# Moving layer 1's last eight conditioning units from layer 0's gate stage to the boundary between the two layers

## The reference, cut to what matters

```python
for l in range(DEPTH):
    mod_l = (silu(c) @ ada_w[l] + ada_b[l])          # 1024 x 6144 weights per layer
    mod_c = (silu(c_ctx) @ ada_w[l] + ada_b[l])
    sh1, sc1, g1, sh2, sc2, g2 = split(mod_l, 6)     # six parts of 1024 columns
    ul = rmsnorm(hl, norm_g[l, 0]) * (1 + sc1) + sh1
    mc, ml = token_mixer(uc, ul, w_in[l], ...)       # input projection, four mixers, gates, output projection
    hl = hl + g1 * rmsnorm(ml, norm_g[l, 1])
    vl = rmsnorm(hl, norm_g[l, 2]) * (1 + sc2) + sh2
    hl = hl + g2 * rmsnorm(ffn(vl), norm_g[l, 3])    # dense SwiGLU in layer 0, 8 experts in layer 1
```

## Time and profile before

| | us |
|---|---|
| median of 3 runs | 2219.38 |
| lowest and highest of them | 2215.46 and 5585.45 |
| the profiled execution, its time | 2221.07 |
| its span in the trace | 2219.2 |
| layer 0's gate stage in the trace, about | 313 to 602 |
| boundary of the layers, last feed-forward matmul to first projection matmul | 1023.1 to 1036.7 |
| TensorE busy | 2135.0 (96%) |
| VectorE busy | 1422.2 (64%) |
| ScalarE busy | 1154.7 (52%) |

### The profile page before, as it was taken

How to read it: one execution, slowest core, us unless ns; L and a number is a source line. 1 busy time by engine, 2 the same in 40 slices (tenths; PEclk the granted TensorE clock), 3 DMA queues, 4 the chain that set the end, 5 groups by cost and what they waited for, 6 DMA issues and landing times. The chain is left out here.

```text
span 2219.2 us, 37036 instructions
## 1 busy us (share of the span) xinstructions
PE 2135.0 (96%) x15402; PEld 1749.0 (79%) x15402; DVE 1422.2 (64%) x1999; ACT 1154.7 (52%) x1588; POOL 142.2 (6%) x117
## 2 busy tenths in 40 slices
PE   6999899999999999998988899999999999999997
PEld 4787687777778888886866799778888888888886
DVE  3546663333452222336567566589999999999998
ACT  4253432322342222325445245478888888888886
POOL 0004420000000000000014400010000000000000
PEclk9999999999999999999989999999999999999999
DMA  6510025665623222221200254489999999999995
GB/s 245 211 79 1 3 98 228 254 259 209 265 102 112 95 95 97 94 94 60 96 1 2 80 210 170 161 311 378 390 380 372 387 381 386 379 381 383 375 412 201
DMA packets 68201, 468.07 MB, mean 211 GB/s; under 512 B 7681, under 2 KB 8641, under 8 KB 14017
## 3 DMA queue, kind: packets, MB, share of 16 engines
q1 hardware_dynamic: 62192, 440.55, 51.7%
q10 hardware_dynamic: 4688, 20.93, 2.5%
q0 software_dynamic: 1152, 4.19, 0.5%
HBM read 453.03 MB, written 12.62 MB: 210 GB/s over the span
## 5 line engine op out<-in xcount | busy, mean ns | idle before, releaser
L2371 DVE TENSOR_TENSOR wsp_l<-ring,wsp_h 128x1024 fp32r<-128x1024 f32 x528 | 643.2, 1224 | 48.0 <-ACT wsp_h L1513 13.3
L1513 ACT CAST wsp_h<-ring 128x1024 fp32r<-128x1024 f32 x528 | 555.5, 1054 | 136.5 <-PE bank L709 80.5
L707 PE MATMUL bank<-wsp_h,xTs_h 128*128 128x512 f32 x704 | 283.5, 403 | 0.4 <-DVE wsp_l L2371 0.4
L709 PE MATMUL bank<-wsp_h,xTs_l 128*128 128x512 f32 x704 | 275.6, 392 | 0.0
L708 PE MATMUL bank<-wsp_l,xTs_h 128*128 128x512 f32 x704 | 274.3, 390 | 0.0
L2946 DVE TENSOR_TENSOR dsp_l<-ring,dsp_h 128x1024 fp32r<-128x1024 f32 x66 | 80.9, 1226 | 234.1 <-ACT dsp_h L2014 234.0
L2014 ACT CAST dsp_h<-ring 128x1024 fp32r<-128x1024 f32 x66 | 69.2, 1048 | 249.7 <-PE bank L1389 175.3
L1281 PE MATMUL bank<-u_hi,gsp_h 128*128 128x512 f32 (+1 forms) x512 | 174.3, 341 | 0.0
L1281 PE MATMUL bank<-x_lo,gsp_h 128*128 128x512 f32 (+1 forms) x512 | 172.1, 336 | 0.0
L1281 PE MATMUL bank<-u_hi,gsp_l 128*128 128x512 f32 (+1 forms) x512 | 171.6, 335 | 0.0
L709 PEld LDWEIGHTS bank<-wsp_h,xTs_l 128*128 128x128 f32 x704 | 132.2, 188 | 29.1
(11 more groups left out here) (374 smaller groups left out, 4160.5 us busy)
## 6 DMA issues: line engine op xcount, KB each, us to landing
ring<-in_moe_tiles_dram SPq DMA_DIRECT2D x264, 1024.0 KB, 7.1
ring<-in_ada_tiles_dram SPq DMA_DIRECT2D x48, 1024.0 KB, 9.3
ring<-in_ffn_tiles_dram SPq DMA_DIRECT2D x33, 1024.0 KB, 4.8
ring<-in_gate_tiles_dram SPq DMA_DIRECT2D x32, 1024.0 KB, 6.3
ring<-in_in_tiles_dram SPq DMA_DIRECT2D x22, 1024.0 KB, 5.4
arena<-in_branch_tiles_dram ACTq DMA_DIRECT2D x8, 1024.0 KB, 7.0
ring<-in_out_tiles_dram SPq DMA_DIRECT2D x8, 1024.0 KB, 4.9
x_rows<-arena SPq DMA_DIRECT2D x1, 3584.0 KB, 16.2
```

What stands on the lines that cost most here:

```text
L707: pe.matmul(o, xTs[0][:, kk, :], whi[:, k, :], start=(kk == 0), stop=False)
L709: mm = pe.matmul(o, xTs[1][:, kk, :], whi[:, k, :], start=False, stop=(kk == KD - 1))
L1513: act.copy(wsp[0][:, g % 4, :], half_slot(MOE0, g)).then_inc(s.gq_o.up, 1)
L2371: v.tensor_tensor(wsp[1][:, g % 4, :], half_slot(MOE0, g), wsp[0][:, g % 4, :], ALU.subtract).then_inc(s.gq_pt.up, 1)
```

## The change

The last group of conditioning units leaves the gate stage. Its tiles stand behind the feed-forward's in `slots`, ahead of layer 1's first projection tile. PE does three of the units between the transposes of tiles 0 and 1, and five between those of tiles 1 and 2, all into bank 4, after waiting that `post_add` has read tile 2 out of it (`po_h2(3)`). Then it waits for `ada_copy` before bank 4 is used for transposes. `ada_columns` of this group follows the first projection tile, `modulate_group` goes to DVE's fifth half tile, and layer 1's transposition of its gate rows goes one projection tile later.

```diff
--- before.py
+++ after.py
@@ -46,6 +46,7 @@
 GROUP = 8
 ADA_BATCH = (3, 3, 2)
 ROW_AT = 17
+LAST_AT = 3
 RING = 6
 LEVELS = 5
 CH = 64
@@ -342,7 +343,7 @@
         def ada_batch(g):
 
             i, j = divmod(g, len(ADA_BATCH))
-            return range(GROUP * i + sum(ADA_BATCH[:j]), GROUP * i + sum(ADA_BATCH[:j + 1])) if i < GROUPS else ()
+            return range(GROUP * i + sum(ADA_BATCH[:j]), GROUP * i + sum(ADA_BATCH[:j + 1])) if i < GROUPS - 1 else ()
 
         def ada_slots(units):
             for u in units:
@@ -375,6 +376,7 @@
             if l == 0:
                 FFN0 = len(slots)
                 slots += [(d["ffn_tiles"][j], (KD, CW) if j < NF else (2, D)) for j in range(3 * NF // 2)]
+                ada_slots(LATE[GROUP * (GROUPS - 1):])
         assert len(ADA_SLOT) == DEPTH * NADA
         MOE0 = len(slots)
 
@@ -455,7 +457,7 @@
         RT_UNITS = [[(a, st, jh) for a in range(2) for st in ((0, 1), (1,))[l] for jh in range(1 + st)] for l in range(DEPTH)]
         SCAN = (tuple(range(2 * NT)), (3, 2, 1, 0, 7, 6, 5, 4))
 
-        ADA_DONE = [2 * len(ADA_BATCH) * (i + 1) + 1 for i in range(GROUPS)]
+        ADA_DONE = [2 * len(ADA_BATCH) * (i + 1) + 1 for i in range(GROUPS - 1)]
 
         def chunk_bank(k):
 
@@ -570,10 +572,18 @@
                         last = transpose(bank[chunk_bank(k)][:, P * t:P * (t + 1)], xs[:, t, P * k:P * (k + 1)])
                     last.then_inc(s.tp1.up, 1)
 
+            def last_units(below, some):
+
+                pe.wait_ge(*below.po_h2(3))
+                for u in some:
+                    ada_products(len(EARLY) + GROUP * (GROUPS - 1) + u, 4, u, GROUP)
+
             def next_T(s, below, g):
 
                 pe.wait_ge(*below.po_h2(2 * g + 2))
                 for i, t in enumerate(PARTS[0][g]):
+                    if g == 0 and i == 1:
+                        last_units(below, range(0, LAST_AT))
                     pe.wait_ge(*s.xs1(t + 1))
                     for b in range(4):
                         for k, c in part_rows(0, g, b):
@@ -790,6 +800,8 @@
                     prenorm_T(s, range(6))
                 else:
                     next_T(s, sig[0], 0)
+                    last_units(sig[0], range(LAST_AT, GROUP))
+                    pe.wait_ge(ada_row, PAIRS + GROUPS)
                     next_T(s, sig[0], 1)
 
 
@@ -878,7 +890,10 @@
                     pe.sem_inc(slot_free, 1)
                     if c0 == OFF_GQA:
                         fourier_rows()
-                    if l and i == 1:
+                    if l and i == 0:
+                        ada_columns(PAIRS + GROUPS - 1, 5, GROUP)
+                    if l and i == 2:
+                        pe.wait_ge(mod_ok, PAIRS + GROUPS)
                         gate_row_transpose(s, l, 4)
 
                 def retention_columns(g):
@@ -1245,7 +1260,7 @@
                         gate_row_transpose(s, l, 3)
                     if i == 3 and j == 0:
                         pe.wait_ge(*s.row_ok(1))
-                    if i and j == 0:
+                    if 0 < i < GROUPS and j == 0:
                         ada_columns(PAIRS + i - 1, 3, GROUP)
                     for u in ada_batch(g):
                         ada_products(len(EARLY) + u, 2, u % GROUP, GROUP)
@@ -1320,7 +1335,7 @@
                         p, hf = i // 2, i % 2
                         n, words = out_part(l, i)
                         if ctx_out and t == 1 and p == 0:
-                            pe.wait_ge(mod_ok, PAIRS + GROUPS)
+                            pe.wait_ge(mod_ok, PAIRS + GROUPS - 1)
                         if t == tiles[0]:
                             pe.wait_ge(*g_wlo(MW + i + 1))
                         lo_ = ring_lo[:, n % RING, words].rearrange("p (k n) -> p k n", k=2)
@@ -1683,6 +1698,7 @@
                             weight_high(j)
                 else:
                     weight_high(0)
+                    ada_copy(PAIRS + GROUPS - 1, 4, len(ADA_SLOT))
                     for b in range(2):
                         next_part(s, 1, b)
                         input_high(2 * b)
@@ -1740,7 +1756,7 @@
                                 dst, src = rows[:, t:t + per, c:c + CW], half[:, 0:per, :]
                             act.copy(dst, src).then_inc(s.win_ok.up, 1)
                             unit += 1
-                            if l and i == 2 and q == 0:
+                            if l and i == 3 and q == 0:
                                 gate_row_out(s, l, 4)
                             if c0 == OFF_GQA and q == 1:
                                 fourier_copies()
@@ -2014,7 +2030,7 @@
                         act.copy(dsp[0][:, q % 3, :], half_slot(FFN0, q)).then_inc(g_whi.up, 1)
 
                 if ctx_out:
-                    act.wait_ge(mod_ok, PAIRS + GROUPS)
+                    act.wait_ge(mod_ok, PAIRS + GROUPS - 1)
                 for i, t in enumerate(tiles):
                     post_tile(i, t)
                     if i == 2:
@@ -2273,12 +2289,12 @@
                     ins = modulation(0, part, bank[7][:, 4 * part:4 * (part + 1)], 2 * j, 2)
                 ins.then_inc(mod_ok, 1)
 
-            def modulate_group(i):
+            def modulate_group(i, columns_at=3):
 
                 v.wait_ge(ada_sum, PAIRS + i + 1)
                 for e in range(2):
                     l, part = (LATE[GROUP * i + PER_PART * e]) // NADA, LATE[GROUP * i + PER_PART * e] % NADA // PER_PART
-                    ins = modulation(l, part, bank[3][:, 16 * e:16 * (e + 1)])
+                    ins = modulation(l, part, bank[columns_at][:, 16 * e:16 * (e + 1)])
                 link(ins)
                 v.sem_inc(mod_ok, 1)
 
@@ -2515,6 +2531,8 @@
                 step = 0
                 for q in range(1 if l else 2, 16):
                     weight_low(q)
+                    if l and q == 4:
+                        modulate_group(GROUPS - 1, 5)
                     if q == 3:
                         v.wait_ge(prm_in[l], 32)
                     for _ in range(CONV_STEPS.get(q, 0)):
@@ -2881,8 +2899,6 @@
                 merged_low(2)
                 merge(MW - 1)
                 merged_low(3)
-                if ctx_out:
-                    modulate_group(GROUPS - 1)
                 output_weight_low(5)
                 merged_low(4)
                 merged_low(5)
```

## The result

The changed kernel takes **2223.28 us** in the median of 20 runs (2215.99 to 2227.51), against 2217.54 us for the kernel before in as many: ratio 1.0023, 95% interval 1.0015 to 1.0032, so 5.1 us slower (3.3 to 7.1). (The medians lie 5.7 us apart; the ratio leaves out the one execution of the kernel before that took 5585.45 us.) That is no change by the 2% of the prediction, and it lies in its range; but it is more than the +2.0 us of the forecast's sum. A later timing gave 1.0033 (1.0020 to 1.0046), 7.3 us slower.

What follows compares the result with a forecast made beforehand. PE (TensorE) was taken as the bound, busy 2135.0 of 2219.2 us. Terms -7.7 + 0.4 + 9.3 = +2.0 us gave 2223.1 on the profiled execution, 2221.4 us as a median; range 2212 to 2226.

Steps and rivals of the forecast that it cites:

- rival C: Clock falls in the PE gap before the first projection tile's second half: 1.9 us lost, net +3.9, 2223.3 us; chance 18%.
- the prediction's own sign: At the layer boundary, a granted clock of 0.50 after the second gap would show rival C true; 1.9 us lost.
- the second gap: PE idle between the first projection tile's halves, waiting for h_keep: forecast 1049.1 to 1053.2, about 4 us.
- The gate stage: Layer 1's gate stage loses three unit batches (7.3 us) and the turning into columns (0.4 us): -7.7 us.
- PE's own work: At the layer boundary, eight units of 0.93 us (7.4 us) fill PE's waits for DVE's norms; almost nothing lost.
- The loads: Ring at the boundary: seventh unit's load lands 4.9 us after issue, later ones 2.45 us apart, projection tile 0 at 1036.1.
- h_keep: Store at the boundary, issued about 1035.3 behind five loads, lands at 1048.6 instead of 1034.1.
- The second half: Second half of the first projection tile waits for h_keep and casts, starting 1053.2 instead of 1043.88: +9.3 us.
- the prediction's own upper bound of 11.3: Largest delay of the projection tile's second half: 9.3 us plus 2 if loads land 2.8 us apart instead of 2.45.
- Columns: Turning the sums into columns now runs after the first projection tile, on the path: +0.4 us.
- Rivals A and B: Boundary: A, h_keep late only by its issue, net -2.1, 20%; B, both transfers early enough, net about -6, 12%.
- The forecast's own narrower range: Whole kernel at 2220 to 2224 us, from a delay of the projection tile's second half of 8 to 11 us.

Runs made afterwards that it cites:

- The first experiment: The changed kernel with h_keep issued behind layer 1's first projection tile, five loads earlier: 2220.78 us, ratio 1.0014 to the kernel before; repeated, 2216.32 us, ratio 0.9996.

## Why the prediction was right, and where it was short

The mechanism was the forecast's, and rival C came on top of it: by the prediction's own sign (0.50 behind the second gap) C is what happened. That C's time, 2223.3, is the measured one to the tenth is luck, as the sums below show. Instants of after stand in the scale of before when the 8.55 us between the two executions' first transposes are added (8.4 of them are the gate stage's).

- **The gate stage: forecast -7.7, measured -8.4.** The 7.7 were summed from the starts of the batches, and these don't show that the products on either side of a batch are also spaced wider than elsewhere, 0.32 and 0.33 us for 0.23. Three batches and the columns make 0.7 of it. The rows before, beside those of the earlier trace rows:

```profile
569.12 0.39 PE L1305 MATMUL bank<-yT_hi,wbr_lo 128*128 128x512 f32 x1
...
572.50 0.39 PE L1281 MATMUL bank<-x_lo,gsp_h 128*128 128x512 f32 x1
```

That nothing else in the gate stage waited for the moved instructions is confirmed: the whole gain arrives.

- **PE's own work: right.** The waits for DVE's norms were filled. PE's new waits for the units' loads, 2.2 us, delay nothing that h_keep doesn't delay more.
- **The loads: the right order and spacing, but 1.3 us more for the first.** The seventh unit's load took 6.2 us, where I took the 4.9 of a lone load. Rows 6 held the better row: the first of several close loads took 6.0. The eighth landed 7.8 us after an issue 0.9 later, 2.4 us behind it, so the 2.45 held.
- **h_keep: forecast 1048.6, measured 1043.1 + 8.55 = 1051.65, 3.05 late.** Of this 1.3 is the first load, and up to tile 3 it stays at 1.45. Nearly all the rest arises between tile 3 and tile 4, which land at 1036.3 (1023.3 + 13.0) and 1040.6, 4.3 us apart and not the 0.3 + 2.5 that I had given the small ab tile and tile 4. My first reading was that the small tile costs this. The run with h_keep early refutes it: there tile 4 lands 2.4 us behind ab (1036.0, 1038.4), and the wide step, with its dip in the rate, is at the transfer that stands ahead of h_keep wherever that is: tile 0 at 1025.8, 4.1 us behind the eighth unit at 1021.7 (4.4 in its repetition; and 4.0 from ab to tile 4 in the changed kernel). So it goes with h_keep's own transfer, of which the forecast's steps had counted only the ordinary 2.45: it costs some 1.6 to 2.0 us more. Why was not tested. From h_keep to the second half is 4.5 us, forecast 4.6.
- **The second half: forecast +9.3, measured +12.3** (from 20.09 us behind the transposes to 32.36). This is the term that was too small, and h_keep's landing is all of the difference. It lies above the prediction's own upper bound of 11.3, whose 2 us were to come from loads 2.8 us apart; they kept to 2.4 to 2.5, but for the one ahead of h_keep. The first experiment ties h_keep down: with it early the second gap is gone and the boundary 6 us shorter.
- **The clock: rival C was counted at 18% as a case of its own, and came true in the forecast's own case, +1.9** (the second half takes 8.07 us with its tail, against 6.15; in the second execution 8.54, from 1044.97). Its condition was that h_keep lands after 1044.5, and the forecast itself put it at 1048.6. So C should have been part of the forecast once the gap was in it; the sum would have been +3.9. Filling the gap gave 1.7 back. The Trainium skill, TensorE: Matmul & The Clock Gate, section Why this matters for your kernels, warns of idle gaps between bursts of matmuls, and the trace agrees: 0.50 in the window from 1046, behind a gap of 5.59 us.
- **Columns: +0.4, right.** Rivals A and B fell: h_keep took 15.1 us, and the first cast waited until 1028.88 + 8.55 = 1037.4.

Together: -8.4 + 12.3 + 1.9 + 0.4 = **+6.2**, against +2.0, and the timings' +5.1 and +7.3. The forecast of 2221.4 is nearer to the measured 2223.28 than that, because it started from a median of three that lay 1.8 us above the later 2217.54. The range held the time by its width and by that offset. The forecast's own narrower range, 2220 to 2224, holds it too, though the delay that it was built on (8 to 11 us) was exceeded: that also is luck.

## What to carry to other kernels

Before moving work into a stretch where the engine waits, follow its loads: idle time of the engine is room for its instructions, but their transfers take places in the ring ahead of those that the next stage needs. Here the boundary grew by 3.7 us with the instructions alone, most of it by the clock, and by 10.5 more with their loads. A store or copy that is issued by its place in a queue of loads moves with the queue; give it a place by when it is needed, and move only so much as the ring covers (four units, with h_keep and the copy in better places, cost nothing at the boundary; eight, with both where they were, cost 14). And when a forecast opens a gap on TensorE, the clock that follows the gap belongs in the same sum.

## What the runs showed of the hardware

- The time from issue to landing of the same 1 MB transfer, h_keep: 3.8 us alone, 3.9 where the units were not loaded, 6.7 and 7.1 with half of them, 10.6 to 11.9 behind one projection tile, 15.1 behind all. In the early version more loads are issued while it is under way, and it still lands first of them, 2.5 us behind tile 0 (1025.8, 1028.4): wherever the traces here give landings, they keep the order of issue.
- The load just ahead of the store of h_keep lands late, 4.0 to 4.4 us behind its forerunner in six executions with the store in two places, where other 1 MB loads land 2.45 apart; the rate falls from 434 to 180 GB/s meanwhile (in the run with h_keep early). The 128 KB tile added 0.3 us.
- The lower clock was left in different ways. In the changed kernel it came back to 1.00 at 1038, with projection products running since 1034.47. With h_keep early it was 0.95 on average from 1030 to 1032, when PE had done nothing but sixteen transposes since 1027.24 (3.39 us) and rested again, as before. But transposes do not always bring it back: in the second execution of the changed kernel sixteen of them, longer still, ended at 0.50, and it stayed there until 1036. So what the prediction says of transposes and the clock holds for the execution that it was read from, and not for every one.

```profile
1027.27 3.68 PE L564 MATMUL bank<-consts,arena 128*128 128x128 f32 x16 [2.70 <-ACT S L1513]
...
1034.00:1036.00 2.00, 1.98 (x5) 1.07 (x4) 1.72 (x4) 0.00 (x0) 0.00 (x0) 0.50 0.97 324
```

- From the start of layer 0's gate stage to the boundary's transposes takes the same time in every execution with the same work there (678.9 us in all seven with eight units moved, 683.3 in both with four), while its start scatters from 329 to 337 us over the executions traced. Over such a stretch lengths between marks resolve tenths, where the total time resolves microseconds. Where PE waits they do not: the boundary gave 40.4 and 41.2 us, and 34.3 and 35.6, and the stretch behind it 234.5 and 237.6, for one kernel each.
